# Selected pages of a sparse-attention decoder fetched as keys and values apart, on two queues

## The reference

```python
s_c = einsum('bqgrd,bngd->bqgrn', qg, kcmp)             # 32 compressed blocks
p_c = masked_softmax(s_c, c_valid);  o_c = p_c @ vcmp
imp = where(forced, FORCE_SCORE, sum(p_c, axis=3))       # importance of each block of 64 rows
_, idx = lax.top_k(imp, 16)                              # 16 blocks are selected
s_s = qg . ks_t[idx];  p_s = masked_softmax(s_s, s_mask);  o_s = p_s @ vs_t[idx]
s_w = qg . wk;         p_w = masked_softmax(s_w, w_valid); o_w = p_w @ wv   # 512-token window
o = g[..., 0:1] * o_c + g[..., 1:2] * o_s + g[..., 2:3] * o_w
```

## Time and profile before

| what | value |
|---|---|
| three executions | 1264.09, 1266.54, 1273.97 us |
| profiled execution | 1272.86 us, span 1271.2 us |
| TensorE (PE) busy | 1186.5 us, 93% of the span |
| VectorE, ScalarE, GpSimd busy | 653.0, 454.1, 166.2 us |
| mean granted TensorE clock | 0.966 of full |
| chain that ended last | PE 79%, DVE 8%, ACT 4%, issue 3%, SPq 3%, DMA 2% |
| q1 (issued by SyncE) | 134.84 MB |
| q0 (issued by GpSimd) | 27.65 MB |

### The profile page before, as it was taken

The page is one execution under the profiler, slowest core; times in us unless marked ns, Lnnn a source line. Parts: engine busy times, 40 slices in busy tenths (PEclk is TensorE's granted clock), DMA queues, the critical chain, the costliest instruction groups (busy, mean ns, idle before and its releaser), DMA issues.

```text
span 1271.2 us, 21848 instructions
## 1 busy us (share of the span) xinstructions
PE 1186.5 (93%) x8421; PEld 1047.8 (82%) x8421; DVE 653.0 (51%) x1178; ACT 454.1 (36%) x724; POOL 166.2 (13%) x276
## 2 busy tenths in 40 slices
PE   6999897989989989899998996999999999999997
PEld 5888686767867757578887896889999999999997
DVE  3549857445666533331253557445543235667663
ACT  3100101023776541420032356545343224555551
POOL 0010011454431222200000002001000000001000
PEclk9999968989999989999999998899999999999998
DMA  6571323454371853844455644364353322232201
GB/s 187 116 233 37 128 48 116 125 132 128 100 179 54 270 148 118 281 131 155 131 179 131 224 153 131 117 232 133 100 166 100 100 89 78 67 100 95 72 1 71
DMA packets 166770, 163.88 MB, mean 129 GB/s; under 512 B 41526, under 2 KB 147859, under 8 KB 166459
## 3 DMA queue, kind: packets, MB, share of 16 engines
q1 hardware_dynamic: 157658, 134.84, 35.2%
q0 software_dynamic: 9008, 27.65, 7.0%
HBM read 154.08 MB, written 12.53 MB: 131 GB/s over the span
## 4 chain that ended last, share of the span: by engine, by line
PE 79%; DVE 8%; ACT 4%; issue 3%; SPq 3%; DMA 2%; POOL 0%; DVEq 0%; ACTq 0%
PE banks L1439 21%; PE banks L996 18%; PE banks L1693 14%; PE banks L1393 4%; PE banks L1179 4%; PE banks L1375 2%; PE banks L1139 1%; PE banks L1214 1%; PE banks L1231 1%; SPq L663 1%; PE banks L1293 1%; DVE rounded L2760 1%; PE banks L1242 1%; PE banks L1137 1%; DMA upper<-in_cache_win_kv 1%
## 5 line engine op out<-in xcount | busy, mean ns | idle before, releaser
L1439 PE MATMUL banks<-rounded 128*128 128x288 f32 (+1 forms) x2304 | 299.0, 290 | 3.8 <-DVE rounded L2806 3.2
L1439 PEld LDWEIGHTS banks<-rounded 128*128 128x128 f32 x2304 | 293.8, 190 | 7.5 <-DVE rounded L2806 4.1
L996 PE MATMUL banks<-arena 128*128 128x256 f32 (+3 forms) x1056 | 255.2, 403 | 7.2 <-DVEq L2166 3.3
L996 PEld LDWEIGHTS banks<-arena 128*128 128x128 f32 (+1 forms) x1056 | 201.6, 193 | 52.8 <-DVEq L2166 3.5
L1693 PE MATMUL banks<-rounded 128*128 128x272 f32 x1536 | 195.1, 290 | 3.8 <-DVE rounded L2987 3.8
L1693 PEld LDWEIGHTS banks<-rounded 128*128 128x128 f32 x1536 | 194.5, 190 | 4.5 <-issue 3.1
L2760 DVE TENSOR_TENSOR rounded<-arena,rounded 128x2048 fp32r<-128x2048 f32 x54 | 125.5, 2324 | 78.1 <-ACT rounded L1884 78.0
L2987 DVE TENSOR_TENSOR rounded<-arena,rounded 128x1088 fp32r<-128x1088 f32 x64 | 82.9, 1304 | 60.2 <-ACT rounded L2127 60.2
L1884 ACT ACTIVATE rounded<-arena 128x2048 fp32r<-128x2048 f32 x54 | 103.0, 1906 | 11.9 <-DMA arena<-in_w_xq 6.8
L2127 ACT ACTIVATE rounded<-arena 128x1088 fp32r<-128x1088 f32 x64 | 71.1, 1114 | 81.0 <-PE banks L1693 79.8
L2920 DVE TENSOR_TENSOR arena<-arena 128x256 f32<-128x256 f32 (+1 forms) x64 | 28.1, 439 | 86.3 <-ACT arena L1969 86.3
(11 more groups left out here) (424 smaller groups left out, 1453.7 us busy)
## 6 DMA issues: line engine op xcount, KB each, us to landing
arena<-in_w_up SPq DMA_DIRECT2D x22, 1024.0 KB, 5.5
arena<-in_w_down SPq DMA_DIRECT2D x16, 1024.0 KB, 5.2
arena<-in_w_in SPq DMA_DIRECT2D x13, 1024.0 KB, 8.9
upper<-in_cache_nsa_kv SPq DMA_DIRECT2D x64, 128.0 KB, 2.7
upper<-in_cache_nsa_kv POOLq DMA_DIRECT2D x64, 128.0 KB, 4.7
arena<-in_w_out SPq DMA_DIRECT2D x8, 1024.0 KB, 7.4
arena<-in_cache_mem_kv SPq DMA_DIRECT2D x16, 512.0 KB, 8.0
arena<-in_cache_nsa_kv SPq DMA_DIRECT2D x90, 64.0 KB, 2.3
```

What stands on the lines that cost most here:

```text
L996: ins = mm(bank(b + h, (NA, NB)[h], rows=M), lhsT(k), rhs[:, k, toks], start=(k == 0), stop=(k == K - 1))
L1439: ins = mm(bank(b, N), w[:, k], a[:, k, toks], start=(k == 0 and z == 0), stop=(k == K - 1 and z == 2))
```

## The change

`sel_pages` gets a parameter `half`: 0 fetches keys (columns 0 to 127), 1 fetches values (128 to 255). Each DMA now carries 64 KB, and there are two for each page. SyncE calls it for the keys of all four blocks of each group, GpSimd for the values of all four blocks. Each call reads its 16 page numbers itself.

The keys' wait in group 1 is now for the scores (`s_mm`) of the block whose place they take; for block 0 it is for all 20 scores of group 0, because the window lies there. The values' wait in group 1 stays `sample_pv`. Group 1 takes its blocks in the order 2, 1, 3, 0, and its window goes where block 2's keys were. SyncE issues `weights(3)` after the keys of the first block of group 0. The window's values move from SyncE to GpSimd, behind the values of block 3, one DMA of 256 KB per sample. All values share one semaphore `v_rows_in`, for which TensorE waits ahead of `pv`; it no longer waits on `kv_in` for values.

```diff
--- before.py
+++ after.py
@@ -298,12 +298,12 @@
         so_sb = place(P, R + 9080)
         s_sel = place(PAST + TS, R + 5176)
         s_win = place(WIN + TS, R + 7256)
-        KC_ORDER = (0, 2, 1, 3, 4)
+        KC_ORDER = ((0, 2, 1, 3, 4), (2, 1, 3, 0, 4))
         KT_BANKS = (0, 1, 4, 5)
 
-        def keys_page(b, kc):
-
-            return kv_pg[:, KV_AT[kc % 4], b, :, 0:P]
+        def keys_page(gg, b, kc):
+
+            return kv_pg[:, KV_AT[KC_ORDER[gg][0] if kc == 4 else kc], b, :, 0:P]
 
         qbd = place(256, R + 25920).rearrange("p (b c) -> p b c", b=DB)
         assert R + 9216 + 4 * PAGES * 256 <= R + 25920 and R + 26176 <= ACOLS
@@ -674,24 +674,23 @@
             src = raw_rows(j).rearrange("p n (g d) -> p (n g) d", g=2)[:, :, half * 32:half * 32 + 32]
             signal(copy(relaid[half][:, :, k * 32:k * 32 + 32], src.rearrange("p n d -> p d n")), f"relaid_{half}")
 
-        def sel_pages(eng, gg, kc, known):
-
-            known.update({(gg * 4 + b, p): page for b in range(4)
-                          for (_, p), page in known_pages(eng, (gg * 4 + b,), kc * 4, kc * 4 + 4).items()})
+        def sel_pages(eng, gg, kc, half):
+
+            known = known_pages(eng, range(gg * 4, gg * 4 + 4), kc * 4, kc * 4 + 4)
             if gg:
-                eng.wait_ge(sem("sample_pv"), 4 * gg)
+                if half == 0:
+                    eng.wait_ge(sem("s_mm"), 4 * KC_ORDER[0].index(kc) + 4 if kc else 20)
+                else:
+                    eng.wait_ge(sem("sample_pv"), 4 * gg)
             elif kc == 0:
                 raw_relaid(eng, 13)
             else:
                 eng.wait_ge(sem("cmp_done"), 2 * CU - (kc == 2))
             for b in range(4):
-                q = gg * 4 + b
-                for i in range(4):
-                    p = kc * 4 + i
-                    page = known[q, p] if (q, p) in known else known_pages(eng, (q,), p, p + 1)[q, p]
-                    eng.dma_start(kv_pg[:, KV_AT[kc], b, i:i + 1, :],
-                                  A["cache_nsa_kv"][0][bass.ds(page, 1), :, 2:4].rearrange("n p z g d -> p n (z g d)"))\
-                        .then_inc(sem(f"kv_in_{kc}"), 16)
+                for p in range(kc * 4, kc * 4 + 4):
+                    eng.dma_start(kv_pg[:, KV_AT[kc], b, p - kc * 4:p - kc * 4 + 1, half * P:half * P + P],
+                                  A["cache_nsa_kv"][0][bass.ds(known[gg * 4 + b, p], 1), :, 2 + half].rearrange("n p g d -> p n (g d)"))\
+                        .then_inc(sem(f"kv_in_{kc}" if half == 0 else "v_rows_in"), 16)
 
         block = ctx.enter_context(nc.Block())
 
@@ -791,11 +790,11 @@
 
             win = A["cache_win_kv"][0]
             for gg in range(NG2):
-                sel_pages(sp, gg, 0, known)
-                if gg == 0:
-                    raw_relaid(sp, 4 * CU - 1)
-                    weights(3)
-                sel_pages(sp, gg, 1, known)
+                for n, kc in enumerate(KC_ORDER[gg][0:4]):
+                    sel_pages(sp, gg, kc, 0)
+                    if gg == 0 and n == 0:
+                        raw_relaid(sp, 4 * CU - 1)
+                        weights(3)
                 if gg == 0:
                     sp.wait_ge(*step("prompt_attn_done"))
                 else:
@@ -803,8 +802,7 @@
                 for b in range(4):
                     w = win[gg * 4 + b].rearrange("(n p) z g d -> z p n (g d)", p=P)
                     sp.wait_ge(sem("s_mm"), gg * 20 + b + 1)
-                    sp.dma_start(keys_page(b, 4), w[0]).then_inc(sem(f"k_win_{b}"), 16)
-                    sp.dma_start(v_win[:, b], w[1]).then_inc(sem("v_win_in"), 16)
+                    sp.dma_start(keys_page(gg, b, 4), w[0]).then_inc(sem(f"k_win_{b}"), 16)
 
             weights(1)
             sp.wait_ge(sem("sample_pv"), 4 * NG2)
@@ -931,11 +929,17 @@
                 if j in (8, 9):
                     known.update(known_pages(pool, (j - 2,), SP_PAGES, PAGES))
             for gg in range(NG2):
-                sel_pages(pool, gg, 2, known)
-                if gg == 0:
-                    pool.wait_ge(sem("cmp2_mm"), CU)
-                    signal(pool.memset(qbd, 0.0), "qbd_zeroed")
-                sel_pages(pool, gg, 3, known)
+                for kc in range(4):
+                    sel_pages(pool, gg, kc, 1)
+                    if kc == 3:
+                        if gg == 0:
+                            pool.wait_ge(*step("prompt_attn_done"))
+                        for b in range(4):
+                            pool.dma_start(v_win[:, b], A["cache_win_kv"][0, gg * 4 + b, :, 1].rearrange("(n p) g d -> p n (g d)", p=P))\
+                                .then_inc(sem("v_rows_in"), 16)
+                    if gg == 0 and kc == 0:
+                        pool.wait_ge(sem("cmp2_mm"), CU)
+                        signal(pool.memset(qbd, 0.0), "qbd_zeroed")
 
             def inverse_rms(n):
 
@@ -1280,7 +1284,7 @@
 
                 for u in range(5 + 1):
                     if u < 5:
-                        kc = KC_ORDER[u]
+                        kc = KC_ORDER[gg][u]
                         for b in range(4):
                             U_ = gg * 20 + u * 4 + b
                             if kc == 4:
@@ -1290,7 +1294,7 @@
                             if U_ >= 4:
                                 pe.wait_ge(sem("kt_out"), U_ - 3)
                             for i in range(4):
-                                ins = pe.transpose(bank(KT_BANKS[b], P, i * P), keys_page(b, kc)[:, i, :], ident)
+                                ins = pe.transpose(bank(KT_BANKS[b], P, i * P), keys_page(gg, b, kc)[:, i, :], ident)
                             signal(ins, "k_used")
                     if u >= 1:
                         n4 = gg * 5 + u - 1
@@ -1301,7 +1305,7 @@
                             pe.wait_ge(sem("s_out"), n4 - 1)
                         for b in range(4):
                             signal(mm(psum[b * 32:b * 32 + 32, 2 + n4 % 2, :], qbd[:, gg * 4 + b, :],
-                                      keys_page(b, KC_ORDER[u - 1]), start=True, stop=True), "s_mm")
+                                      keys_page(gg, b, KC_ORDER[gg][u - 1]), start=True, stop=True), "s_mm")
                 for br in range(2):
                     for b in range(4):
                         ins = mm(psum[b * 32:b * 32 + 32, 6, 128 + br * 32:160 + br * 32], qbd[:, gg * 4 + b, :],
@@ -1335,8 +1339,8 @@
                             ins = pe.transpose(bank(b_, P, i * P), s_win[:, i * P:(i + 1) * P], ident)
                     signal(ins, "ps_T")
                 pe.wait_ge(sem("ps_out"), gg * 6 + 6)
-                pe.wait_ge(sem("v_win_in"), 64 * (gg + 1))
                 pe.wait_ge(sem("pcs_out"), gg + 1)
+                pe.wait_ge(sem("v_rows_in"), 16 * 68 * (gg + 1))
                 def pv(b, p, v, start=False, stop=False):
 
                     return mm(psum[b * 32:b * 32 + 32, 7, 256:384], p[:, b * 32:b * 32 + 32], v, start=start, stop=stop)
@@ -1843,8 +1847,8 @@
                 for u in range(20):
                     U_ = gg * 20 + u
                     act.wait_ge(sem("k_used"), U_ + 1)
-                    b, kc = u % 4, KC_ORDER[u // 4]
-                    signal(fn(keys_page(b, kc), bank(KT_BANKS[b]).rearrange("p (n k) -> p n k", n=4), ACT.Copy), "kt_out")
+                    b, kc = u % 4, KC_ORDER[gg][u // 4]
+                    signal(fn(keys_page(gg, b, kc), bank(KT_BANKS[b]).rearrange("p (n k) -> p n k", n=4), ACT.Copy), "kt_out")
                 act.wait_ge(sem("sel_max"), gg + 1)
                 signal(fn(s_sel, s_sel, ACT.Exp, bias=sst[:, 2:3], accum_out=sst[:, 3:4]), "sel_exp")
                 signal(fn(s_win, s_win, ACT.Exp, bias=sst[:, 4:5], accum_out=sst[:, 5:6]), "sel_exp")
@@ -2655,7 +2659,7 @@
                 dve.wait_ge(sem("pc_s_ready"), gg + 1)
                 signal(ts(pcs, pcs, gs[:, gg, 0:1], None, ALU.mult), "pcg_ready")
 
-                for u, kc in enumerate(KC_ORDER):
+                for u, kc in enumerate(KC_ORDER[gg]):
                     dve.wait_ge(sem("s_mm"), gg * 20 + u * 4 + 4)
                     ps = bank(2 + (gg * 5 + u) % 2)
                     if kc < 4:
```

## The result

The changed kernel took 1298.85 us (median of 4, 1296.66 to 1301.41) beside 1268.69 us (median of 4, 1264.09 to 1273.97) for the kernel before: a ratio of 1.0237, 95% interval [1.0189, 1.0285], so 30.2 us slower. A second set of runs gave 1299.68 beside 1266.66 us, 1.0274 [1.0244, 1.0304], 33.0 us. The forecast was 1299.9 us, made of a median of 1266.5 for the kernel before and a cost of 33.4 us.

The account below looks back on a forecast made before the run. TensorE's own work was taken to bound the kernel (79% of the chain). Group 1's values 30.8 us later plus 2.6 for the clock made 33.4; on the median of 1266.5, 1299.9 us, range 1286 to 1313 (its own 1289 to 1311).

Parts of the forecast that it names:

- The pace of a block: On each queue, 9.1 us of loads and 8.85 us of issues, with the seams 18.2 us between first issues.
- Start of group 0's keys: SyncE in group 0: blocks 2, 1 and 3 follow the weights from 426.54 us; block 3 landed at 483.3.
- Group 0's delay: Group 0: scores end 13.5 us later, with 2.6 us for the clock 16.1 us late; values cost nothing.
- Group 1's race: Group 1: SyncE's keys allow `pv` at 580.9; GpSimd's values end last at 583.8, 30.8 us later than 553.04.
- some 13: Sign: TensorE waits some 13 us for keys ahead of group 0's fourth block and again ahead of group 1's.
- a few: Sign: TensorE waits a few us for values ahead of group 1's `pv`.
- The clock: TensorE at half clock behind stalls: 2.6 us ahead of group 0's scores and 2.6 us once more in group 1.
- The range: Around the forecast time: its own range 1289 to 1311 us; with part of both slower rivals, 1286 to 1313.
- Cheap loads: Rival on the queues: loads overlap four at a time, a block costs 11.2 us, time 1260.3 us; chance 0.06.
- Bandwidth: Rival: half-size pieces cap the DMA engines, issues stretch by 10% or so, together 1310 us; chance 0.09.
- Half the price: Rival: group 1's delay is hidden, group 0's isn't, so 16.1 us are added, 1282.6 us; chance 0.05.
- The early start wins nothing: Group 1: keys that no longer wait for `pv` win nothing, since values are late.

Follow-up runs that it names:

- busy_stall: The changed kernel with 44 idle-filling matmuls of 128x256 on TensorE ahead of its wait for group 1's values; 1312.68 us, ratio 1.0341 to the kernel before.
- busy_stall_20: The changed kernel with 20 filling matmuls of 128x256 ahead of TensorE's wait for group 1's values; 1298.24 us, ratio 1.0231 to the kernel before.
- one_load: The changed kernel, but each call reads one page number and uses it for all its 16 DMAs; 1262.02 us, ratio 0.9958 to the kernel before.
- late_keys: The changed kernel, but group 1's keys wait for group 0's `pv` as the values do; 1311.08 us, ratio 1.0318 to the kernel before.
- numbers_kept: The kernel before, but in group 1 each queue reads its 32 page numbers once, then issues keys and later values from them; 1268.06 us, ratio 0.9993.

## Why the prediction was right, step by step

The mechanism was right: each queue does its loads and issues one after the other, twice as many as before, and TensorE waits for them. The path through it was not that of the prediction in group 0, and the closeness of the total is in part luck. Along the chain that ended last, the longer stretch adds up like this:

| step | forecast, us | measured, us |
|---|---|---|
| group 0's `pv` ends later | 16.1 | 12.5 |
| from there to the start of group 1's `pv` | 14.7 | 19.0 |
| group 1's `pv` itself (clock) | 2.6 | 3.2 |
| sum | 33.4 | 34.7 |

- **The pace of a block**, 18.2 us: SyncE 17.4 and 17.7, GpSimd 19.1 twice and once 21.4, with a pause of 3.25 us inside a block that I had not foreseen and can't explain. Prices of a load and of an issue: confirmed one by one (0.57, 0.56).
- **Start of group 0's keys.** I took the weights' 7.50 us from the earlier trace rows; behind pages of half the size they took 3.60, 3.9 us less. Block 3's transposes began 25.9 us into the stretch for 31.2. The stall ahead of them was 11.2 us. The prediction speaks of one of 13 us, but its own moments, 483.3 and 467.05, give 16.3; 13.5 is the delay of the scores, less because the window waits go.
- **Group 0's delay.** Scores ended 34.5 us into the stretch for 24.8: +9.7 for a predicted 16.1 with the clock. The values, said to cost nothing with 6 us of cover, came last by 1.85 us and made the delay 10.8. So the path of group 0 was GpSimd's values and not SyncE's keys; this step of the prediction was wrong.
- **Group 1's race.** The right chain won. `pv` began 132.4 us into the stretch for 100.9: +31.5, for 30.8 forecast. But the keys' chain was ready 11 us ahead of the values, not 3: SyncE started earlier and ran quicker than taken, GpSimd slower. TensorE so waited 6.0 us (9.3 in the second profile) for keys and 11.2 for values, where "some 13" and "a few" were to be seen. Two errors of some 4 us cancelled: group 0's `pv` ended 3.6 us less late than forecast, and GpSimd then took 4.3 us more than forecast. The total is better than its terms.
- **The clock.** Two episodes of 2.6 us were taken, one in block 3's transposes of group 0 and one in group 1's `pv`. The rows have 1.7 us more in block 3's transposes (3.67 for 1.97), 1.7 in group 0's `pv`, 2.8 in group 1's first 32 transposes (6.45 for 3.69), 1.4 in its fourth block and 3.2 in its `pv`. But only the two `pv` are on the chain: behind the slow transposes TensorE waits for values anyway. That makes 4.9 us for the 5.2 taken, a right size with one of the two places wrong. Group 0's part isn't firm: its `pv` took 7.03 and 6.98 us in the two profiles, but 5.37 and 5.44 in busy_stall and busy_stall_20, which are the same up to there. The Trainium skill (TensorE: Matmul & The Clock Gate, Part 1: The HAM clock gate) calls the ramp under 1% of a span. 4.9 of 1295 us is 0.4%, so the trace agrees, but it is a seventh of what the stretch got longer.
- **The range.** Its upper end, 1311, isn't the sum of its terms: 1299.9 + 4 + 5 is 1308.9. The lower end is (1289.7).
- **The base.** The forecast stood on 1266.5 us for the kernel before. With the 1268.69 us measured beside the result it would have been 1302.1, so the agreement within 1.1 us is closer than that of the costs, 33.4 for 30.2 and 33.0.
- **The rivals.** Cheap loads: the loads did cost, and one_load shows that without them the time is 1262.0, where I had 1260.3. Bandwidth: not seen; 64 KB pages were issued at 8.63/16 = 0.54 us each and landed sooner than those of 128 KB. Half the price: not seen.
- **"The early start wins nothing"** failed by 12 us, as late_keys shows. Values were last only because the keys had started early.

## What to carry to other kernels

Count what a queue does between its DMAs. A transfer with a page number from memory costs its queue a load and an issue, here 0.57 + 0.56 us, whatever its size between 64 and 128 KB; splitting transfers and reading the numbers on both queues doubles both. If a split is wanted so that one half can start earlier, read the numbers once, in idle time, keep them in registers, and let one queue issue both halves. numbers_kept splits group 1 in this way and loses nothing against the kernel before, but no gain of it alone is shown either. And when two engines feed a third, find which of them comes last: the longest wait on TensorE, for keys, wasn't the one that set the time.

## What the runs showed of the hardware that was not expected

- Three 1 MB weight DMAs took SyncE 7.50 us to issue behind its 16 pages of 128 KB and 3.60 behind 16 of 64 KB. Over the other runs it was 4.78 to 6.87 us where the pages were 128 KB or two halves, and 2.80 to 3.00 where each was one half of 64 KB, but 4.96 in one_load. So the size behind which they queue isn't all of it; the cause stays open.
- GpSimd paused for 3.25 us between two page DMAs at 541.6 to 544.9 with nothing to wait for. It lies behind the third page of block 2, and all six other profiles of kernels that issue all values so have a pause there, of 3.00 to 4.14 us. The cause stays open.
- One filling matmul of 128x256 in float32 took 0.44 us (8.90/20).
